# Two transformer layers and a mixer block on one core: the rotary rows of queries and keys are gathered by loads from SBUF to SBUF and turned on VectorE, and the split of the convolution's taps is changed

## The reference

```python
h = rmsnorm(x, norm_mix[l])
q, k, v, u, ug, ga, gb = jnp.split(h @ w_in[l], SPLITS, axis=-1)
q = partial_rope(rmsnorm(q, q_norm[l]), cos, sin)   # 16 heads of 64
k = partial_rope(rmsnorm(k, k_norm[l]), cos, sin)   # 2 heads of 64
a_out = sliding_window_attention(q, k, v, sinks[l])
c_out = conformer_conv(u, ug, ...)                  # 31 taps on 512 channels
merged = sigmoid(ga) * a_out + sigmoid(gb) * c_out
x = x + merged @ w_out[l]                           # then a gated FFN

def partial_rope(x, cos, sin):                      # ROT_DIM = 16 of 64 channels
    x1, x2, xp = x[..., :8], x[..., 8:16], x[..., 16:]
    return concatenate([x1*cos - x2*sin, x2*cos + x1*sin, xp])
```

## Time and profile before

| | |
|---|---|
| median of 3 runs | 2224.13 us (2224.1 to 2224.35) |
| the profiled execution, its own time | 2225.23 us |
| its span, from first to last instruction | 2223.4 us |
| PE busy | 2204.8 us |
| DVE busy | 1201.9 us |
| ACT busy | 995.9 us |
| POOL busy | 1089.6 us |
| mean granted TensorE clock | 0.999 |

### The profile page before, as it was taken

The page is one execution under the profiler, slowest core; times in us unless marked ns, Lnnn a source line. Parts: engine busy times, 40 slices in busy tenths (PEclk is TensorE's granted clock), DMA queues, the critical chain, the costliest instruction groups (busy, mean ns, idle before and its releaser), DMA issues.

```text
span 2223.4 us, 29331 instructions
## 1 busy us (share of the span) xinstructions
PE 2204.8 (99%) x10507; PEld 1769.5 (80%) x10509; DVE 1201.9 (54%) x1550; ACT 995.9 (45%) x1573; POOL 1089.6 (49%) x545
## 2 busy tenths in 40 slices
PE   9999999999999999999999999999999999999999
PEld 7877788888888877778888888887787678888887
DVE  6887863222345887875222344858887746333301
ACT  5567743322224558743333214436645654444311
POOL 5973344444443983244444443433666753444442
PEclk9999999999999999999999999999999999999999
DMA  5221232333672222132333473322221012333332
GB/s 171 93 67 65 60 95 88 100 95 94 201 223 84 88 76 67 51 92 85 95 99 98 151 237 107 101 86 67 67 86 57 29 48 85 105 96 100 96 95 85
DMA packets 59990, 216.04 MB, mean 97 GB/s; under 512 B 6784, under 2 KB 7040, under 8 KB 59904
## 3 DMA queue, kind: packets, MB, share of 16 engines
q1 hardware_dynamic: 52416, 187.62, 27.7%
q10 hardware_dynamic: 7488, 27.27, 3.6%
HBM read 212.76 MB, written 2.10 MB: 97 GB/s over the span
## 4 chain that ended last, share of the span: by engine, by line
PE 91%; DVE 4%; ACT 2%; issue 1%; POOL 1%; ACTq 0%; POOLq 0%; DVEq 0%
PE bank L1658 27%; PE bank L1660 27%; PE bank L1659 27%; PE bank L1921 1%; PE bank L1849 1%; ACT prob L593 1%; POOL soft_lo L419 1%; PE bank L1895 1%; PE bank L1737 1%; PE bank L1732 1%; PE bank L2204 1%; PE bank L2215 0%; DVE conv L1227 0%; PE bank L2248 0%; DVE prob L1141 0%
## 5 line engine op out<-in xcount | busy, mean ns | idle before, releaser
L343 POOL TENSOR_TENSOR wl<-raw,wh 128x1024 fp32r<-128x1024 f32 x349 | 856.5, 2455 | 1005.9 <-ACT wh L475 1005.8
L1658 PE MATMUL bank<-hh,wh 128*128 128x512 f32 (+1 forms) x1984 | 780.1, 393 | 6.4 <-ACT root L809 2.1
L1660 PE MATMUL bank<-hh,wl 128*128 128x512 f32 (+1 forms) x1984 | 765.2, 386 | 0.0
L1659 PE MATMUL bank<-hl,wh 128*128 128x512 f32 (+1 forms) x1984 | 764.7, 385 | 0.0
L475 ACT ACTIVATE wh<-raw 128x1024 fp32r<-128x1024 f32 x351 | 369.7, 1054 | 568.6 <-PE bank L1660 511.4
L1658 PEld LDWEIGHTS bank<-hh,wh 128*128 128x128 f32 x1984 | 373.4, 188 | 94.6 <-issue 14.5
L1659 PEld LDWEIGHTS bank<-hl,wh 128*128 128x128 f32 x1984 | 373.6, 188 | 77.8 <-issue 5.0
L1660 PEld LDWEIGHTS bank<-hh,wl 128*128 128x128 f32 x1984 | 373.4, 188 | 75.7
L1658 PE MATMUL bank<-ah,wh 128*128 (+1 forms) x512 | 201.7, 394 | 0.0
L1660 PE MATMUL bank<-ah,wl 128*128 (+1 forms) x512 | 200.7, 392 | 0.0
L1659 PE MATMUL bank<-al,wh 128*128 (+1 forms) x512 | 198.7, 388 | 0.0
(11 more groups left out here) (381 smaller groups left out, 2851.8 us busy)
## 6 DMA issues: line engine op xcount, KB each, us to landing
raw<-stream SPq DMA_DIRECT2D x351, 512.0 KB, 3.6
ada_w<-ada ACTq DMA_DIRECT2D x48, 512.0 KB, 4.6
x<-x_t ACTq DMA_DIRECT2D x4, 512.0 KB, 7.5
out_t<-x SPq DMA_DIRECT2D x8, 256.0 KB, 2.1
cst<-consts SPq DMA_DIRECT2D x1, 640.0 KB, 6.8
tmp<-masks SPq DMA_DIRECT2D x1, 320.0 KB, 7.1
par<-params SPq DMA_DIRECT2D x1, 249.0 KB, 5.7
cst<-consts SPq DMA_DIRECT2D x1, 224.0 KB, 4.8
```

Source lines behind the costliest of these rows:

```text
L343: nc.gpsimd.tensor_tensor(wl[:, slot, :], raw[:, raw_slot, :], wh[:, slot, :].bitcast(F32), ALU.subtract).then_inc(lo_ready, 1)
L1658: mm(dst, wh[:, slot, w], xh, start=start, stop=False)
L1659: mm(dst, wh[:, slot, w], xl, start=False, stop=False)
L1660: return mm(dst, wl[:, slot, w], xh, start=False, stop=stop)
```

## The change: what it does

The channels within a tile of two heads are put in another order by the host (`turned_pairs`), so that the 32 channels to turn stand together on partitions 48 to 79. ACT copies each q tile from PSUM to `q` with its gain, and squares it without waiting for DVE. PE's swap products, all 9 in a layer, and DVE's two products and subtraction for each q tile are gone.

SP loads the 32 rows of a tile into `th` (`take_rows`), and in four more loads the same rows with the halves of each pair exchanged. Four tiles make a full set of 128 rows: batch 0 is k, q0, q1, q2; batch 1 is q3 to q6; batch 2 is q7 alone. DVE turns a batch in three operations (`turn_rows`), and SP loads the rows home (`rows_home`). PE waits for them ahead of scores 0, 4 and 12. These loads stand in SP's list among the refills of `raw`, so the loop of refills is opened in the q, v and first gate chunks.

Tile 0 of the convolution is now all DVE's (31 taps instead of 11). ACT and POOL keep tile 1: 31 products and 30 additions in a layer, where there were 51 and 49.

```diff
-        TAPS_U, TAPS_Q = [2, 3, 4, 2, 4, 5], [5, 4, 3, 4, 5, 5, 5, 5]
-        SPLIT = 20
-        PRODUCTS = [(0, j) for j in range(SPLIT)] + [(1, j) for j in range(TAPS)]
...
+        TAPS_U, TAPS_Q = [3, 4, 4, 4, 4, 5], [6, 6, 7, 8, 8, 5, 7, 7]
+        N_ADDS = TAPS - 1
...
+        R_AT, R_ROWS = 48, 32
+        R_TILES = [[KT, 0, 1, 2], [3, 4, 5, 6], [7]]
...
+            def take_rows(l, t):
+                b, i = R_BATCH[t]
+                sp.wait_ge(lin_free, M_LAYER * l + (M_Q[t] if t < KT else M_KSPREAD) + 1)
+                if b == 2:
+                    sp.wait_ge(rows_back[0], 16 * len(R_TILES[0]) * (l + 1))
+                at = i * R_ROWS
+                sp.dma_start(rows_of(b, i), rotary(t, 0, R_ROWS)).then_inc(rows_in[b], 16)
+                for n in range(4):
+                    sp.dma_start(other_rows[b % 2][at + 8 * n:at + 8 * n + 8, :], rotary(t, 8 * (n ^ 1), 8)).then_inc(rows_in[b], 16)
+
+            def rows_home(l, b):
+                sp.wait_ge(turned_rows, 3 * l + b + 1)
+                for i, t in enumerate(R_TILES[b]):
+                    sp.dma_start(rotary(t, 0, R_ROWS), rows_of(b, i)).then_inc(rows_back[b], 16)
...
+                for t in range(KT):
+                    refill(c0 + C_Q + t + ahead)
+                    take_rows(l, t)
+                    if t == 2:
+                        take_rows(l, KT)
+                    if t == 5:
+                        rows_home(l, 0)
+                refill(c0 + C_V + ahead)
+                rows_home(l, 1)
+                refill(c0 + C_GATE + ahead)
+                rows_home(l, 2)
...
+                    act.wait_ge(lin_free, m0 + M_Q[t])
+                    af(q[:, t, :], bank[:, M_Q[t] % 4, :], ACT.Copy, scale=par_l(l, "qk_gain", 1 + t)).then_inc(lin_free, 1)
...
-                own = [(0, j) for j in range(SPLIT, TAPS)] + [(t, j) for t in (2, 3) for j in range(TAPS)]
+                own = [(t, j) for t in (0, 2, 3) for j in range(TAPS)]
...
+                def turn_rows(b):
+                    n = R_ROWS * len(R_TILES[b])
+                    own_rows, others = rows[b % 2][0:n, :], other_rows[b % 2][0:n, :]
+                    dve.wait_ge(rows_in[b], 16 * 5 * len(R_TILES[b]) * (l + 1))
+                    tt(own_rows, own_rows, cos[0:n, :], ALU.mult)
+                    link(tt(others, others, sin[0:n, :], ALU.mult))
+                    tt(own_rows, own_rows, others, ALU.add).then_inc(turned_rows, 1)
...
-                    stt(tmp[:, 4 + t % 2, :], bank[:, M_Q[t] % 4, :], gain, sin, ALU.mult, ALU.mult)
-                    stt(q[:, t, :], bank[:, M_Q[t] % 4, :], gain, cos, ALU.mult, ALU.mult).then_inc(lin_free, 1)
-                    if t:
-                        turned_q(t - 1)
...
-                    swap_q(t - 1)
```

More of the change, by code:

```diff
@@ L179, in build @@
         lin_free = stage("lin_free")
-        k_wide, k_spread, k_swapped, k_ready, q_swapped = (stage(n) for n in ("k_wide", "k_spread", "k_swapped", "k_ready", "q_swapped"))
+        k_wide, k_spread, turned_rows = (stage(n) for n in ("k_wide", "k_spread", "turned_rows"))
+        rows_in, rows_back = [stage(f"rows_in{b}") for b in range(3)], [stage(f"rows_back{b}") for b in range(3)]
         half_tanh, glu_ready, vt_turned = (stage(n) for n in ("half_tanh", "glu_ready", "vt_turned"))
@@ L303, in build, with rows_of, rotary @@
         norm1_shift = [bank[:, (MB + 2 + u % 2) % 4, half_cols[u // 2]] for u in range(4)]
+        rows, other_rows = [th[:, 0, 2 * i, :] for i in range(2)], [th[:, 0, 2 * i + 1, :] for i in range(2)]
+        def rows_of(b, i):
+            return rows[b % 2][i * R_ROWS:(i + 1) * R_ROWS, :]
+        def rotary(t, first, n):
+            at = slice(R_AT + first, R_AT + first + n)
+            return k[at, :] if t == KT else q[at, t, :]
         def group(g):
@@ L323, in _, with refill @@
             sp.dma_start(tmp[:, 4:6, :].rearrange("p a t -> p (a t)")[:, 0:5 * P], masks).then_inc(masks_in, 16)
[L324 to L329, removed]
+            def refill(c):
@@ L330, in _, with refills @@
                 sp.wait_ge(lo_ready, c - RR + 1)
                 sp.dma_start(raw[:, c % RR, :], stream[c]).then_inc(raw_in[c % RR], 16)
+            def refills(first, end):
+                passes = (end - first) // RR
+                with sp.Fori(0, passes) as i:
+                    for s in range(RR):
+                        sp.wait_ge(lo_ready, i * RR + (first + s - RR + 1))
+                        sp.dma_start(raw[:, (first + s) % RR, :], stream[bass.ds(i * RR + (first + s), 1)].rearrange("a p n -> p (a n)")).then_inc(raw_in[(first + s) % RR], 16)
+                for c in range(first + passes * RR, end):
+                    refill(c)
@@ new lines, in rows_home @@
+            def rows_home(l, b):
+                sp.wait_ge(turned_rows, 3 * l + b + 1)
+                for i, t in enumerate(R_TILES[b]):
+                    sp.dma_start(rotary(t, 0, R_ROWS), rows_of(b, i)).then_inc(rows_back[b], 16)
+            done = 2 * RR
+            for l in range(DEPTH):
+                c0 = l * C_LAYER
+                ahead = RW + RR
+                refills(done, c0 + C_Q + ahead)
+                for t in range(KT):
[9 more added lines that the diff above has]
+                rows_home(l, 2)
+                done = c0 + C_GATE + 1 + ahead
@@ L332, in _ @@
+            refills(done, N_CHUNKS)
             for t in range(KT):
@@ L370, in _ @@
                 rests(done, c0 + C_U + 2 + RW)
-                p = 0
+                added = 1
                 for i in range(C_U + 2, C_GATE + 16):
@@ L375, in _ @@
                     adds = ADDS_AT.get(i, 0)
-                    while adds and p < len(PRODUCTS):
-                        adds -= add_tap(l, p)
-                        p += 1
+                    for j in range(added, added + adds):
+                        add_tap(l, j)
+                    added += adds
                 done = c0 + C_GATE + 16 + RW
@@ L574, in gate @@
                     act.wait_ge(gate_free, 16 * l + g + 1)
+                    if g == 8:
+                        for b in (1, 2):
+                            act.wait_ge(rows_back[b], 16 * len(R_TILES[b]) * (l + 1))
                     if g == 12:
```

117 lines of the change are left out of this document (43 added, 74 removed).

## The result

| | before | changed |
|---|---|---|
| median of 13 runs each | 2224.99 us (2224.1 to 2226.39) | 2229.63 us (2227.49 to 2231.26) |
| the profiled execution, its own time | 2225.23 us | 2229.34 us |
| its span | 2223.4 us | 2227.6 us |
| mean granted TensorE clock | 0.999 | 0.995 |

What follows compares the result with a forecast made beforehand. PE's stream of products was taken as the bound. Per layer, 15.05 us less 14 us of turns on DVE left a gain of 1.05, 2.1 in all: 2224.1 - 2.1 = 2222.0 us, range 2211 to 2231.

Steps and rivals of the forecast that it cites:

- DVE late, clock kept: Main case: DVE's second gate delays scores(1), PE keeps full pace; 2222.0 us, 2217 to 2226, chance 0.35.
- the clock falls in the stall: Rival: PE runs at half pace behind the wait at scores(1), 5.0 us more in two layers; 2227.0 us, chance 0.22.
- S: Time of a layer's three turns on DVE, nine operations, ahead of the second gate; taken as 14 us, bounds 6 and 18.6.
- Swaps, 0.85 us each on PE: PE's swap products in the q, k stage: removing nine a layer frees 7.65 us, 15.3 us in all.
- DVE is the last at `scores(1)`: At scores(1), PE waits for DVE's second gate instruction, a stall of 6.6 us in each layer.
- k's multiplication at 80.05: DVE's multiplication of k in layer 0 starts at 80.05 instead of 81.75, since two swaps ahead of it are gone.
- S = 14: The three turns of a layer on DVE take 14 us, between 12.8 and 15.0 by their places beside POOL's work.
- The mean over the four rows of before: Mean of four like DVE operations in k's rotation of the kernel before, 1.72 us each, giving 15.5 for nine.
- The gain of a layer, 15.05 - S: At scores(1), which moves from 138.42 to 123.37 + S in layer 0: a gain of 1.05 us a layer.
- The clock, put at nothing: Behind the stall at scores(1), the main case took PE's clock as kept, with no added time.
- Loads, refills, trips home at no cost: SP's loads in the q stage: issues 0.48 us apart, rows landing within 3.6 us, nothing waits for them.
- The taps that leave POOL can only help.: Convolution taps moved from POOL to DVE can only help the weights' rests on POOL; no size given.

Runs made afterwards that it cites:

- e2: The changed kernel with 36 unused products put on PE between scores(0) and scores(1), where it waits: 2225.79 us, ratio 1.0001 to the kernel before.
- e5: The changed kernel with ACT's copy of k placed one channel tile earlier, ahead of q2's: 2228.23 us, ratio 1.0009 to the kernel before.
- e1: The changed kernel with the second input of all turn operations read from PSUM instead of SBUF (wrong values): 2210.62 us, ratio 0.9931 to the kernel before.
- e3: The changed kernel with 12 taps of channel tile 0 given back to ACT and POOL: 2223.5 us, ratio 0.9989 to the kernel before.
- e7: The kernel before with only DVE's additional taps, the rotary turns left as they were: 2228.72 us, ratio 1.0016 to the kernel before.
- e4: The changed kernel with the three turns of a layer made by GpSimd instead of DVE: 2210.64 us, ratio 0.9931 to the kernel before.
- e6: The changed kernel with DVE's taps between the turns and the second gate moved behind that gate: 2220.46 us, ratio 0.9976 to the kernel before.

## Why the prediction was right or wrong

The time lies in the range (2211 to 2231), but that range was wide, and the likeliest case, "DVE late, clock kept" (2222.0, with 2217 to 2226 around it), is not what happened: the kernel got slower and not faster. Two steps failed. DVE reached the second gate later than reckoned, which ate the gain (with the clock kept, in e2, the kernel is as fast as before), and the clock, taken as kept, fell, which made it a loss. The rival "the clock falls in the stall" is what happened, with a later gate. Its 2227.0 is nearer in part by luck, because its price for the clock was too high (5.0 for 3.7) and its S too low.

- **Swaps, 0.85 us each on PE.** Right: periods of 6.39 and 6.40 us.
- **DVE is the last at `scores(1)`.** Right, in both layers, released by the second gate. The stall was forecast as 6.6 us; 8.0 were measured there and 0.6 ahead of `scores(0)`.
- **k's multiplication at 80.05, "DVE is there in time".** Off by 0.83: it waited for ACT's copy of q2, whose place among the reads of PSUM is ahead of k's. I had looked only at whether DVE and PE were ready. Without that copy in its way (e5) it starts at 80.38.
- **S = 14: the first step that failed, with k's start.** The sum gave the gate at 122.45 + 14 = 136.45; it came at 138.91, of which 1.5 us is S = 15.5 and 0.83 is k. The mean over the four rows of before gave 15.5 and so did the measurement; I went below it on the guess that POOL can't slip in where DVE's next operation is ready at once. It does: two of the three operations of the second turn took 1.78 and 1.67 us with no gap between them. The rows of before showed it already: in both layers the second of the two operations followed the first without a gap and took 1.67 us. The mechanism itself, operations with two SBUF inputs against POOL's instructions, is confirmed by e1. The Trainium skill's rule (SBUF — State Buffer, Who interferes with whom), that the two exclude each other for a whole instruction, agrees with the 2.94 us at 93.41.
- **The gain of a layer, 15.05 - S.** Forecast +1.05; measured -1.24 and, in layer 1, 822.69 - 826.44 + 2.80 = -0.95.
- **The clock, put at nothing: the second step that failed.** e2 shows that it isn't kept: 3.7 us by the traces, 4.0 by the ratios, where the rival had 5.0. The reason given for keeping it, that no row of the kernel before shows a fall behind a pause, is false: its trace shows one at 1381.85, behind 1.79 us of wait, and between 1380 and 1385 us its granted clock is 0.71. The prediction had half pace only at the start of the program. Its extent, 12 products, was taken from the start of the program and was too long: behind the wait the two of `scores(1)`, its eight short ones and some three full ones ran slow. Here the rule of the Trainium skill (TensorE: Matmul & The Clock Gate, Part 1), that an idle array goes back to 1.2 GHz, agrees with the trace, 0.42 us from start to start behind 8.02 us of wait.
- **Loads, refills, trips home at no cost.** Right for the changed kernel: no row shows a wait for them. But the issues of the rows' loads took 0.66 us each and not 0.48 (five from 82.57 to 85.85), so that k's left from 85.85 to 89.1, for a turn that began at 93.41. It was close: in e3, where SP's list was held up, the turn waited 2.51 us for its rows.
- **"The taps that leave POOL can only help."** On POOL, yes (e3 shows what they do there); but e7 shows the price of the same taps on DVE, where nothing else is taken from it, 3.6 us.

For the profiled execution the forecast was 2223.1, and it took 2229.34, 6.2 us more. The late gate is (1.05 + 1.24) + (1.05 + 0.95) = 4.3, the half pace 3.7, and 1.7 came back behind, 1.0 at the gates that PE waited for before and 0.7 in the second block: together 6.3. Against 2222.0 the median of 2229.63 is 7.6 high, also because the base stood 0.9 higher (2224.99 against 2224.13).

The 0.28 us that PE is late at the very first head sums are there from the start of the program on: PE waits 0.39 us at 10.24 for ACT's rounding of a chunk and stands 0.29 behind the kernel before, where the same product starts at 9.95. Why that chunk is later stays open.

## What to carry to other kernels

Work that is moved off a full engine must be costed at the place where it lands, with its operands in the places where they will be: operations that read PSUM at 0.7 us each were replaced by ones that read SBUF twice, at 1.6 to 2.9 us beside a busy GpSimd. If GpSimd has the time, give it those operations (e4), or let one input come from PSUM. Where PE is the bound and a stall is unavoidable, count the half pace that may stand behind it, and order the list so that the instruction that frees PE's bank is ahead of work that nobody waits for (e6, 0.4% for moving two lines).

## What the hardware showed that I had not expected

- In all these traces POOL, with work at hand, gets its turn between two of DVE's operations with two SBUF inputs, also when they are issued back to back: the second and third operation of a turn never took less than 1.64 us. So three in a row cost 4.2 to 6.3 us, not one delay and then 0.6 each, and a start only 0.5 us earlier (e5) saves 1.1 us.
- The number of partitions doesn't matter for it: on 32 of them the operation behind a rest took 2.82 us and the one behind an addition 1.64, on 128 of them 2.94 and 1.65.
- The clock fell behind waits of 3.0, 4.95 and 8.0 us (e6, e3, the changed kernel), and a longer wait doesn't cost more: 1.55 and 2.71 us behind the two of 3.0, 2.44 behind the one of 4.95 (136.97 to 152.03, 15.06), 2.02 and 1.68 behind those of 8.0. After one of the shortest of these PE ran at full pace for 1.6 us first. A fall can therefore stand behind the wait, where it looks like slow products and not like idle time.
- It also fell behind waits of 1.42 us (e7), 1.71 us (the changed kernel, 1706.07) and 1.79 us (the kernel before, 1381.85), and it didn't behind waits of 1.40, 1.71 and 1.79 us at the same places of the program in another layer or in the other kernel's trace. So the length of a wait doesn't tell by itself, and one trace without a fall at a place is no proof for the next execution. This is also a part of the scatter of one kernel's times: beside e5 to e7, the executions of the kernel before with a mean granted clock of 1.0 took 2224.23 to 2224.57 us, and those with 0.998 took 2226.13 to 2226.61.
